# A feed-forward's input handed over channel-major, and small rows handed over as columns

## The reference, cut to what matters

```python
def rms_norm(x, g):
    xf = x.astype(jnp.float32)
    y = xf * lax.rsqrt(jnp.mean(xf * xf, axis=-1, keepdims=True) + EPS)
    return (y * g.astype(jnp.float32)).astype(x.dtype)

def swiglu(h, w_gu, w_down):
    gate, up = jnp.split(h @ w_gu, 2, axis=-1)
    return (jax.nn.silu(gate) * up) @ w_down

h = swiglu(rms_norm(x, ffn1_pre[l]), ffn1_w_gu[l], ffn1_w_down[l])
x = x + 0.5 * rms_norm(h, ffn1_post[l])
...
```

## Time and profile before

| | us |
|---|---|
| median of three runs | 955.44 (955.23 to 955.62) |
| the profiled execution | 956.07 |
| its span, first to last instruction | 954.3 |
| TensorE busy | 943.6 (99%) |
| VectorE busy | 660.0 (69%) |
| ScalarE busy | 611.3 (64%) |
| GpSimd busy | 108.7 (11%) |
| mean granted TensorE clock | 0.998 |

### The profile page before, as it was taken

How to read it: one execution, slowest core, us unless ns; L and a number is a source line. 1 busy time by engine, 2 the same in 40 slices (tenths; PEclk the granted TensorE clock), 3 DMA queues, 4 the chain that set the end, 5 groups by cost and what they waited for, 6 DMA issues and landing times.

```text
span 954.3 us, 14314 instructions
## 1 busy us (share of the span) xinstructions
PE 943.6 (99%) x5183; PEld 802.1 (84%) x5183; DVE 660.0 (69%) x821; ACT 611.3 (64%) x1050; POOL 108.7 (11%) x149
## 2 busy tenths in 40 slices
PE   8999999999999999999999999999999999999997
PEld 7888888887888888888889789889999898888886
DVE  5665655576666555657679798795666668787887
ACT  6777776666666767686657586555454475665654
POOL 4680000010110000000100913000000010000000
PEclk9999999999999999999999999999999999999999
DMA  9965656543346565565546253334653527465541
GB/s 307 295 204 177 218 176 219 179 151 135 109 160 240 176 212 184 192 204 177 184 134 199 78 177 114 112 135 140 223 190 108 177 92 236 157 219 177 198 154 44
DMA packets 110179, 166.03 MB, mean 174 GB/s; under 512 B 5748, under 2 KB 84884, under 8 KB 110004
## 3 DMA queue, kind: packets, MB, share of 16 engines
q1 hardware_dynamic: 108104, 160.45, 50.1%
q0 software_dynamic: 1872, 4.93, 1.7%
q10 hardware_dynamic: 160, 0.07, 0.0%
HBM read 164.38 MB, written 1.05 MB: 173 GB/s over the span
## 4 chain that ended last, share of the span: by engine, by line
PE 95%; ACT 2%; DVE 2%; DMA 1%; issue 0%; SPq 0%; POOL 0%; POOLq 0%; DVEq 0%
PE ps L2211 26%; PE ps L2213 25%; PE ps L2212 25%; PE ps L2501 6%; PE ps L2507 3%; PE ps L2254 1%; PE ps L2971 1%; DMA raw<-in_ffn_w_gu 1%; PE ps L2644 1%; PE ps L2235 1%; PE ps L2627 1%; PE ps L2907 1%; PE ps L2304 0%; PE ps L2305 0%; DVE arena L1758 0%
## 5 line engine op out<-in xcount | busy, mean ns | idle before, releaser
L1460 DVE TENSOR_TENSOR w_lo<-raw,w_hi 128x2048 fp32r<-128x2048 f32 (+2 forms) x142 | 321.8, 2276 | 82.3 <-ACT w_hi L650 82.3
L650 ACT ACTIVATE w_hi<-raw 128x2048 fp32r<-128x2048 f32 (+2 forms) x142 | 267.0, 1889 | 41.6 <-PE ps L2213 31.0
L2211 PE MATMUL ps<-w_hi,xT_pair 128*128 128x512 f32 (+2 forms) x722 | 275.3, 381 | 1.4 <-DVE w_lo L1472 1.3
L2213 PE MATMUL ps<-w_hi,xT_pair 128*128 128x512 f32 (+2 forms) x722 | 270.8, 375 | 0.0
L2212 PE MATMUL ps<-w_lo,xT_pair 128*128 128x512 f32 (+2 forms) x722 | 270.3, 374 | 0.0
L2211 PEld LDWEIGHTS ps<-w_hi,xT_pair 128*128 128x128 f32 x722 | 135.9, 188 | 27.3 <-DVE w_lo L1472 2.4
L2213 PEld LDWEIGHTS ps<-w_hi,xT_pair 128*128 128x128 f32 x722 | 135.8, 188 | 24.4
L2212 PEld LDWEIGHTS ps<-w_lo,xT_pair 128*128 128x128 f32 x722 | 136.0, 188 | 22.7
L855 ACT ACTIVATE arena<-arena 32x128 f32<-32x128 f32 x288 | 88.4, 307 | 3.2
L2212 PE MATMUL ps<-w_lo,hT_hi 128*128 128x512 f32 x224 | 87.2, 389 | 0.0
L2213 PE MATMUL ps<-w_hi,hT_lo 128*128 128x512 f32 x224 | 87.2, 389 | 0.0
(11 more groups left out here) (376 smaller groups left out, 1319.8 us busy)
## 6 DMA issues: line engine op xcount, KB each, us to landing
raw<-in_ffn_w_gu SPq DMA_DIRECT2D x84, 512.0 KB, 4.6
raw<-in_ffn_w_down SPq DMA_DIRECT2D x44, 512.0 KB, 4.0
raw<-in_w_ffn_up SPq DMA_DIRECT2D x44, 512.0 KB, 4.7
raw<-in_w_in SPq DMA_DIRECT2D x34, 512.0 KB, 4.5
raw<-in_w_out SPq DMA_DIRECT2D x24, 512.0 KB, 4.2
raw<-in_w_ffn_down SPq DMA_DIRECT2D x22, 512.0 KB, 4.2
raw<-in_w_mem_k SPq DMA_DIRECT2D x8, 512.0 KB, 4.0
raw<-in_w_mem_v SPq DMA_DIRECT2D x8, 512.0 KB, 4.3
```

What stands on the lines that cost most here:

```text
L650: act.activation(w_hi[HOME[k]][:, 0:n], raw[k % RING][:, 0:n], ACT.Copy).then_inc(rounded, 1)
L1460: TTn(w_lo[HOME[k]][:, 0:n], raw[k % RING][:, 0:n], w_hi[HOME[k]][:, 0:n].bitcast(F32), ALU.subtract).then_inc(resid, 1)
L2211: pe.matmul(out_, lh, rh, start=first, stop=False, **kw)
L2213: return pe.matmul(out_, ll, rh, start=False, stop=last, **kw)
```

## The change

The host now lays out x channel-major, `x_columns` (128 channels x 8 blocks x 256 tokens, with f0's gain in front), and packs all other gains and taps as ready columns, `columns`. The kernel's first chunk takes input and weights block by block: block r's 128 x 256 input and its 128 x 512 weights are loaded beside each other (input blocks 0 and 1 on ScalarE's queue, the rest on SyncE's), GpSimd rounds the weights of blocks 0 to 3, ScalarE those of 4 to 7 and all input blocks, VectorE takes the rests. TensorE does both token tiles for each block, into banks 4 and 5. No block of X is turned, and the identity and the token-major X (needed for the squares, the residual sum and the turn of chunk 0's activations) are loaded after unit 2, before unit 3. Units 2, 3 and 4 are split in halves; ScalarE's squares stand between the halves of unit 2 and those of unit 3. The warm-up has eleven matmuls. The sixteen loads of rows, the four transposes of `small_columns` and ScalarE's copy become one load of `columns` on GpSimd's queue.

The diff, cut:

```diff
+def packed_columns(inputs):
+    cols = np.concatenate([np.asarray(inputs[n]).reshape(-1, P) for n, _ in COLUMNS]).T
+    gain = np.asarray(inputs["ffn1_pre"]).reshape(KT, P).T
+    x = np.asarray(inputs["x"])[0].reshape(S, KT, P).transpose(2, 1, 0).reshape(P, KT * S)
+    return np.ascontiguousarray(cols), np.ascontiguousarray(np.concatenate([gain, x], axis=1))
...
 SyncE, feed_forward
                 load(u + 2, gate_up(u + 2, gu, 0, 1))
+                if name == "f0":
+                    for t in range(TT):
+                        sp.dma_start(X[:, t, :], a["x"][0].rearrange("(t p) n -> p t n", p=P)[:, t, :]).then_inc(x_ident_in, 16)
+                    sp.dma_start(cst[:, 0:P], consts[:, 0:P]).then_inc(x_ident_in, 16)
                 load(u + 3, gate_up(u + 3, gu, 1, 1))
...
-            sp.dma_start(X[:, 0, :], xv[:, 0, :]).then_inc(x_in[0], 16)
-            load(0, gate_up(0, a["ffn1_w_gu"][0], 0, 0))
-            sp.dma_start(X[:, 1, :], xv[:, 1, :]).then_inc(x_in[1], 16)
-            load(1, gate_up(1, a["ffn1_w_gu"][0], 1, 0))
+            first_weights(0, piece_in[0])
+            first_weights(1, piece_in[1])
+            first_x(2, 1, piece_in[2])
+            first_weights(2, piece_in[2])
+            first_x(3, 1, weights_in[0])
+            first_weights(3, weights_in[0])
+            first_x(4, 2, pieces45_in)
+            first_weights(4, pieces45_in)
+            first_weights(5, pieces45_in)
+            first_x(6, 2, x67_in)
+            first_weights(6, weights_in[1])
+            first_weights(7, weights_in[1])
...
 ScalarE
-            act.dma_start(cst[:, 0:P], consts[:, 0:P]).then_inc(ident_in, 16)
-            act.dma_start(rows_f0[:, :], a["ffn1_pre"][0].rearrange("(r n) -> r n", n=P)).then_inc(ident_in, 16)
+            act.dma_start(xin[:, 0:KT + S], x_columns[:, 0:KT + S]).then_inc(piece_in[0], 16)
+            act.dma_start(xin_k(1), x_columns[:, KT + S:KT + 2 * S]).then_inc(piece_in[1], 16)
...
+            def first_hi(r):
+                pieces_there(r)
+                act.activation(xT_hi[:, r, :], xin_k(r), ACT.Copy, scale=xin_gain[:, r:r + 1]).then_inc(first_rounded, 1)
+                if r >= 4:
+                    c = slice(512 * (r - 4), 512 * (r - 3))
+                    act.activation(w_hi[1][:, c], raw[1][:, c], ACT.Copy).then_inc(first_rounded, 1)
...
+                                    act.wait_ge(x_ident_in, 16 * (TT + 1))
+                                    act.wait_ge(unit_used, 1)
...
+                    for r in range(KT):
+                        first_hi(r)
+                    for part in range(2):
+                        split_half(2, part)
+                    squares(name)
+                    for part in range(2):
+                        split_half(3, part)
...
 GpSimd
+            for r in range(4):
+                pool.wait_ge(piece_in[r] if r < 3 else weights_in[0], 32)
+                nc.gpsimd.tensor_copy(w_hi[0][:, 512 * r:512 * r + 512], raw[0][:, 512 * r:512 * r + 512]).then_inc(pool_rounded, 1)
...
+            pool.dma_start(cols[:, :], columns).then_inc(small_in, 16)
...
 VectorE
+            def first_lo(r):
+                k, c = r // 4, slice(512 * (r % 4), 512 * (r % 4) + 512)
+                dve.wait_ge(first_rounded, x_hi_n(r))
+                STT(out=xT_lo[:, r, :], in0=xin_k(r), scalar=xin_gain[:, r:r + 1], in1=xT_hi[:, r, :].bitcast(F32),
+                    op0=ALU.mult, op1=ALU.subtract).then_inc(first_resid, 1)
...
+                TTn(w_lo[k][:, c], raw[k][:, c], w_hi[k][:, c].bitcast(F32),
+                    ALU.subtract).then_inc(resid if r % 4 == 3 else first_resid, 1)
...
 TensorE, first_units
+                for r in range(KT):
+                    hi, lo = wt(r // 4, 512 * (r % 4), 512)
+                    if r < 4:
+                        pe.wait_ge(first_rounded, x_hi_n(r))
+                        pe.wait_ge(pool_rounded, r + 1)
+                    else:
+                        pe.wait_ge(first_rounded, x_hi_n(r) + 1)
                     for t in range(TT):
+                        pe.matmul(ps[:, 4 + t, :], xT(r, t)[0], hi, start=(r == 0), stop=False)
+                    pe.wait_ge(first_resid, x_lo_n(r))
+                    for t in range(TT):
+                        pe.matmul(ps[:, 4 + t, :], xT(r, t)[1], hi, start=False, stop=False)
...
+                    for t in range(TT):
+                        last = pe.matmul(ps[:, 4 + t, :], xT(r, t)[0], lo, start=False, stop=(r == KT - 1))
...
-            def small_columns():
-                pe.wait_ge(rows_in, 16 * (len(ROWS) + 3))
-                for i, n in enumerate(ROW_TILES):
-                    last = pe.transpose(ps[:, 3, COL_AT[i]:COL_AT[i] + n], rows[0:n, i, :], ident_n(n))
-                last.then_inc(cols_ps, 1)
...
-            for _ in range(9):
+            for _ in range(11):
                 pe.matmul(ps[:, 7, 0:P], xs[:, 1, 0:P], xs[:, 1, 0:P], start=True, stop=True)
-            pe.wait_ge(ident_in, 32)
-            pe.transpose(ps[:, 3, 0:KT], rows_f0[:, :], ident_n(KT)).then_inc(cols_ps, 1)
```

More of the change, by code:

```diff
@@ L176, in constants, with two_blocks @@
     return c, np.stack([q, k]).reshape(2, 2, MH * S)
-def two_blocks(nc, a, consts, mla_rows, out):
+def two_blocks(nc, a, consts, mla_rows, columns, x_columns, out):
     with ExitStack() as ctx:
@@ L269, in view, with xin_k @@
             return v
-        rows = view(0, 4, P)
+        xin = view(5120, KT + KT * S)
+        xin_gain = xin[:, 0:KT]
+        def xin_k(k, n=1):
+            return xin[:, KT + k * S:KT + (k + n) * S]
         act_in = view(0, TT, 512)
@@ L425, in kts, with x_lo_n, x_hi_n @@
             i = NIDX[name]
-            return sum(kt_of(n) * (TT if n in BY_TILE else 1) for n, _ in NORMS[:i]) + k
-        def f0_turned(t, k):
-            return kts("f0", k // 4 * KT + t * 4 + k % 4 + 1)
+            return sum(kt_of(n) * (TT if n in BY_TILE else 1) for n, _ in NORMS[1:i]) + k
+        def x_lo_n(r):
+            return 2 * r + 1 - (r > 3)
+        def x_hi_n(r):
+            return r + 1 if r < 4 else 2 * r - 3
         def turn_at(name, t, k):
@@ L528, in load @@
                 for i, (dst, src) in enumerate(dst_src):
[L529 to L532, removed]
+                    half = isinstance(c, int) and i < 2
+                    sp.dma_start(dst, src).then_inc(half2_in if half and k == 2 else half3_in if half and k == 3 else
+                                                    weights_in[k % RING], 16)
             def rows_by_cols(k, w, row_tile, nk, c0, n):
@@ L545, in gate_up @@
                 dst = raw[k % RING][:, :].rearrange("p (k g n) -> p k g n", k=4, g=2)
[L546 to L549, removed]
+                if k in (2, 3):
+                    return [(dst[:, i:i + 2, g], src[:, 4 * half + i:4 * half + i + 2, g, FC:2 * FC])
+                            for i in (0, 2) for g in range(2)]
                 return [(dst[:, :, g], src[:, 4 * half:4 * half + 4, g, bass.ds(c * FC, FC)]) for g in range(2)]
@@ L769, in chunk @@
                 fc = f * NCH + (peeled if peeled is not None else 2)
-                if peeled != 0 and not (conv and peeled == 1):
+                if peeled != 0 and not (f in (0, 2) and peeled == 1):
                     split(k + 2, j)
@@ L2292, in first_units @@
                             last.then_inc(gu_ps, 1)
+                    if r % 4 == 3:
+                        last.then_inc(unit_used, 1)
             def first_chunk(name, k, done0=None):
@@ L2408, in gate_up @@
                 for half in range(2):
-                    if k == 2 and half == 0:
-                        pe.wait_ge(first_resid, 5)
+                    if k == 2:
+                        pe.wait_ge(first_resid, x_lo_n(KT - 1) + 1 + half)
                     else:
@@ L2413, in gate_up @@
                     for t in range(TT):
-                        if between is not None and half == 0 and t == 1:
+                        if between is not None and half == (1 if k == 2 else 0) and t == 1:
                             between()
@@ L3116 @@
     arrays, aps = {}, {}
+    packed = {n for n, _ in COLUMNS} | {"ffn1_pre"}
     for name in _NAMES:
+        if name in packed:
+            continue
         v = np.ascontiguousarray(inputs[name])
@@ L3121 @@
     fixed = []
-    for name, v in zip(("shape_constants", "mla_mask_rows"), constants()):
+    for name, v in zip(("shape_constants", "mla_mask_rows", "columns", "x_columns"), constants() + packed_columns(inputs)):
         arrays[name] = v
@@ L3125 @@
     out = nc.dram_tensor("out", (1, S, D), F32, kind="ExternalOutput").ap()
[L3126 removed]
+    two_blocks(nc, aps, *fixed, out)
     r = run_bass_kernel_spmd(nc, [arrays], core_ids=[0])
```

229 lines of the change are left out of this document (89 added, 140 removed).

## The result

The kernel after took **959.42 us** (median of five runs, 958.77 to 959.89) against 955.49 (955.23 to 956.37) for the kernel before: a ratio of 1.0040, 95% interval 1.0029 to 1.0052. It is slower by 3.9 us where I had forecast a gain of 2.9. The profiled execution after took 958.77, with a span of 957.0 us against 954.3.

What follows compares the result with a forecast made beforehand. TensorE's own sequence was taken as the bound (95% of the chain). An earlier start (2.3 us) plus removed transposes (0.65) gave 2.93: profiled 956.07 to 953.1, median 952.5; range 951.4 to 953.5, eight in ten 950.7 to 954.9.

Steps and rivals of the forecast that it cites:

- Start, warm-up, landings: Chunk 0: eleven warm-up calls end at 5.78, block 0 starts then, 2.2 us sooner; blocks land from 4.3 to 13.4.
- Turn-taking of GpSimd and VectorE: Chunk 0, blocks 0 to 3: POOL's casts alternate with VectorE's operations, 1.78 us each instead of 1.36, ending at 12.2.
- The sign of "about 1 us" before block 4: Chunk 0: TensorE would show a gap of about 1 us before block 4, ended by ACT's rounding.
- Block 4, units 2 and 3, squares: Early chunks: block 4 at 12.3, unit 2 at 18.0, squares near 19.8, unit 3 at 24.65, down unit at 30.6.
- Small rows' transposes: Last chunk, near 168 us: four transposes of small rows go, 1.10 us becoming two pitches (0.45), a gain of 0.65 us.
- Unit 5 ... lands near 29 to 30.5; I price it at nothing, with 0.7 as the bound: Chunk 2: unit 5's load, issued before the constants, costs nothing, or 0.7 us if it shares engines evenly; residue needed by 36.0.
- POOL issues sixteen row transfers fewer: GpSimd's list: sixteen fewer issues, constants now starting near 23.5 instead of 17.8, beside units 5 and 6.
- All later work follows TensorE's sequence, so it should persist: After the first down unit: the 2.3 us gained at the start would last through the rest of the kernel.
- The median: Final step: the profiled execution was 0.63 above the median of 955.44, so profiled 953.1 became a median of 952.5.
- C: Gain given back: X lands at 22.1 or chunk 2 starves, only 0.65 us remains; median 954.8, chance 0.24.
- D: Slower: smaller pieces and the extra megabyte lower the DMA rate, X lands at 25.9, net loss 3.2; median 958.6, chance 0.06.

Runs made afterwards that it cites:

- list-late kernel: Kernel after, GpSimd's whole list of small loads held back by one wait until VectorE's ninth residue: 953.29 us, ratio 0.9978.
- The four kernels that start as before: Kernel before with: packed columns (960.54 us); those and GpSimd's list held back (954.87); 2.1 MB of unused loads (959.60); twelve unused small broadcasts (956.20).
- the two kernels with the list out of the way: Kernel after with GpSimd's small loads all held back to residue 9 (953.29 us), or given out in four pieces behind residues 9 to 18 (953.23 us).
- the kernel with twelve more rows: Kernel before plus twelve broadcasts of unused small rows (84 KB) behind the shape constants on GpSimd's queue: 956.20 us, ratio 1.0007.
- The columns alone: Kernel before with only the 16 small-row loads and their four transposes replaced by one load of packed columns: 960.54 us, ratio 1.0054.
- small rows late: Kernel after with only positions, sinks and head rows (about 30 KB) held back behind the gain row and a wait: 956.13 us, ratio 1.0009.
- more bytes in the kernel before: Kernel before plus four unused loads of 0.52 MB each (2.1 MB) behind the shape constants on GpSimd's queue: 959.60 us, ratio 1.0038.

## Why the prediction was wrong

- **Start, warm-up, landings: right.** The first product came at 5.74 (5.78 forecast). The blocks were rounded from 4.95, 5.93, 7.20, 8.70, 11.45 and 13.66, against landings forecast at 4.3 to 13.4, each within 0.7 us. One slip in the sum: 16.4 + 3.2 is 19.6, not the 19.8 written for X's landing.
- **Turn-taking of GpSimd and VectorE: priced too high, and covered.** GpSimd's timeline shows casts that took 0.61 in the earlier trace rows at 1.03 to 1.17 when VectorE's operations on two SBUF inputs ran beside them. But TensorE's blocks started 1.4 to 1.5 us apart (5.74, 7.20, 8.66, 10.05), not 1.78, and block 3 ended at 11.58, nearer the 11.2 without turn-taking than the 12.2 that I took. The sign of "about 1 us" before block 4 belongs to 11.2 too; with 12.2 it would have been 0.1.

```profile
4.98 0.61 POOL L1374 CAST w_hi<-raw 128x512 fp32r<-128x512 f32 x1 [4.01 <-DMA raw<-in_ffn_w_gu]
5.96 1.09 POOL L1374 CAST w_hi<-raw 128x512 fp32r<-128x512 f32 x1 [0.37 <-DMA raw<-in_ffn_w_gu]
7.23 1.17 POOL L1374 CAST w_hi<-raw 128x512 fp32r<-128x512 f32 x1 [0.18 <-DMA raw<-in_ffn_w_gu]
```

- **Block 4, units 2 and 3, squares: right.** A gap of 0.95 ended by ScalarE's rounding at 12.53 (12.3 forecast); unit 2 at 18.12 (18.0); the squares at 19.41 (19.8); unit 3 at 23.86 (24.65); the down unit at 29.90 (30.6). The start gained 2.97 against the profiled execution, not 2.3.
- **Small rows' transposes: right.** 0.68 us, seen between chunks 9 and 10 of every kernel without them.
- **"Unit 5 ... lands near 29 to 30.5; I price it at nothing, with 0.7 as the bound": this step failed.** It was rounded from 31.96, and unit 6, which has no term in the sum, from 40.22 against a need of 34.5. Together they cost 5.8 us. Even unit 5's need was set half a us too late: I asked only that its residue be finished before the first product, but that product also waits for the gated product of chunk 1 (L1658), which stands behind that residue in VectorE's list. I had called the list's new place by name and then judged it by when it is issued and by its bytes. Both were too kind: the bytes alone (2.3 MB, 6.6 us) pass unit 6's slack in the list-late kernel of 34.5 - 31.1 = 3.4 us, and the small rows take engine time beyond their bytes. The view was there in the trace of the kernel before: its DMA rows from 31 to 35 us show GpSimd's queue at 39.5% of the engines for 0.03 MB. I had read the rate of the earlier trace rows, where only q1 moves data, in packets of 1 KB; the 168 packets of q0 here average 0.2 KB.

```profile
q1 hardware_dynamic: 338, 0.70, 53.0%
q0 software_dynamic: 168, 0.03, 39.5%
```

- **"POOL issues sixteen row transfers fewer": booked as nothing, worth a loss.** The sixteen issues of 0.51 us kept the rest of the list from being issued before 26.8 us. Taking them away in the kernel before cost 5.1 us.
- **"All later work follows TensorE's sequence, so it should persist": failed for 22 us.** An early start of 2.97 us also moves each later need forward by 2.97, and what is late then was on time before. Chunk 2 had to be walked through like chunk 0. From 52 us on the sentence holds but for the half us below.
- **The median: a second slip, of 0.6 us.** I took 2.93 from the profiled 956.07 and then another 0.63 because that execution lay above its median. The four kernels that start as before have chunk 0's first SiLU 0.50 to 0.62 sooner than that profile, so its excess lay in the start, which the change replaces. Without the second step the forecast for the change without its harm is 953.1; the two kernels with the list out of the way took 953.3 and 953.2. Part of that agreement is luck: the start gained up to 0.7 us more than forecast, and as much was lost again at chunk 4 or after chunk 10 (below).
- **The rivals and the range.** C named a starved chunk 2 but let it only cancel the gain, and nothing holds it there; that set the range's upper end, 954.9, and left 959.4 outside. D is on the right side by another road: its place (X's landing) and its cause (a lower rate of the smaller pieces) did not come about, the squares were early. Its 958.6 lies near 959.4 by luck.

What stays open: 0.4 to 0.7 us that the kernels with the channel-major input lose between chunk 10's SiLU and their last matmul and the others don't (after, from +2.25 to +2.72 against the kernel before); the part of the small rows' price that the engines' time doesn't show; and what share of it is their number of pieces and what their repeated source.

## What to carry to other kernels

A list of loads that nobody waits for soon still has a place in time: when work is taken out from between them, ask what they will now run beside, and price small or broadcast loads not by bytes but at least by the share of the DMA engines that the trace shows for them. A gain at the start moves every later need forward, so follow the loads until the first one with slack greater than the gain. And when a removed step was slow, look at what its slowness kept apart.

## What was not expected of the hardware

Some 80 KB on GpSimd's queue can fill the engines for 2 us: in the kernel with twelve more rows the stretch from 24 to 26 us moved 43 GB/s at a DMA share of 0.83, and 0.08 MB on that queue had 81.1% of the engines.

TensorE's clock fell to half after some gaps and not after others. The columns alone, after 3.47 us of idleness (us, busy of PE, PEld, DVE, ACT, POOL, granted clock, DMA share, GB/s):

```profile
42.00:43.00 1.00, 1.00 (x5) 0.81 (x4) 1.00 (x2) 0.55 (x2) 0.83 (x3) 0.67 0.70 191
43.00:44.00 1.00, 1.00 (x3) 0.77 (x3) 1.00 (x1) 0.96 (x4) 1.00 (x1) 0.50 1.01 269
44.00:45.00 1.00, 1.00 (x4) 0.75 (x3) 0.81 (x1) 0.95 (x5) 1.00 (x1) 0.50 1.00 346
45.00:46.00 1.00, 1.00 (x5) 0.76 (x3) 0.00 (x0) 0.96 (x4) 0.75 (x4) 0.62 0.64 224
```

These four us at 0.67, 0.50, 0.50 and 0.62 of the clock lose 1.7 us, most of the 2 us by which that kernel missed its sum. With small rows late, after 1.91 us of idleness, the clock was 0.50 (1.2 GHz) from 40 to 42 us, and 0.53 and 0.76 in the us on either side, 1.7 us lost as well; with unit 5's lateness of 2.6 us and the start's 2.97 that makes +1.4, as measured. With more bytes in the kernel before, after 2.36 us, it stayed at 1.00:

```profile
40.00:42.00 2.00, 2.00 (x6) 1.51 (x6) 2.00 (x1) 1.93 (x7) 0.00 (x0) 0.50 1.04 348
```

```profile
40.00:42.00 2.00, 1.71 (x7) 1.42 (x8) 1.34 (x3) 0.66 (x1) 0.84 (x4) 1.00 1.02 401
```

So a gap can cost more than its length, by up to 1.7 us here, and the length of the gap alone doesn't tell when: between 28 and 58 us none of the other kernels' gaps, up to 2.36 us, was followed by a lower clock.
